# Placing the gates of 256 tokens in a token-by-expert table: element scatters by GpSimd in place of one-hot matmuls

## What is computed

```
u = take(u_tab, expert)                       # (tokens, 8, 16, 2048)
act = gelu(einsum('cd,chkd->chk', x, u))
wgt = gate * act
y = einsum('chk,chkd->cd', wgt, take(v_tab, expert))
x = LN(alpha * x + y)
```

## Time and profile before

| | |
|---|---|
| median of 3 runs | 4104.31 us (4087.92 to 4105.97) |
| the profiled execution's own time | 4092.33 us |
| its span | 4090.4 us |
| mean granted PE clock | 0.974 of full |
| U sweep, first to last Gelu | 2452.2 to 3280.7 us |
| V sweep | 3281 to about 4060 us |
| PE, DVE, ACT, POOL busy | 94%, 67%, 34%, 29% |

### The profile page before, as it was taken

The page is one execution under the profiler, slowest core; times in us unless marked ns, Lnnn a source line. Parts: engine busy times, 40 slices in busy tenths (PEclk is TensorE's granted clock), DMA queues, the critical chain, the costliest instruction groups (busy, mean ns, idle before and its releaser), DMA issues.

```text
span 4090.4 us, 61953 instructions
## 1 busy us (share of the span) xinstructions
PE 3847.7 (94%) x24631; PEld 3529.6 (86%) x24631; DVE 2760.7 (67%) x3403; ACT 1394.6 (34%) x1975; POOL 1181.8 (29%) x595
## 2 busy tenths in 40 slices
PE   7899999999888999999999899999998879999997
PEld 7789999999877788888888799999998867777776
DVE  3444455554675555666555478888887879989889
ACT  4444444443313300000000244466663323433332
POOL 0000000000533344444444262212113334435542
PEclk9899999999999999999999899999999999999998
DMA  4235554455367699999999447999999999999996
GB/s 166 83 107 182 185 184 179 182 184 185 135 260 286 248 402 396 391 406 395 403 397 404 191 160 288 378 366 366 369 364 408 411 400 406 411 400 406 382 399 264
DMA packets 209831, 1240.23 MB, mean 303 GB/s; under 512 B 20176, under 2 KB 53024, under 8 KB 65824
## 3 DMA queue, kind: packets, MB, share of 16 engines
q1 hardware_dynamic: 125024, 663.85, 42.5%
q0 software_dynamic: 73728, 536.90, 32.2%
q10 hardware_dynamic: 10944, 37.75, 2.3%
HBM read 1200.68 MB, written 37.75 MB: 303 GB/s over the span
## 4 chain that ended last, share of the span: by engine, by line
PE 76%; DMA 10%; DVE 8%; ACT 3%; issue 2%; SPq 0%; ACTq 0%; POOL 0%; DVEq 0%
PE dense_ps L850 22%; PE dense_ps L839 12%; PE dense_ps L841 12%; PE dense_ps L840 12%; DMA wbuf<-in_peer_v_dram 5%; PE dense_ps L1046 5%; PE dense_ps L878 3%; DVE h L1084 3%; DMA row<-in_peer_v_dram,expert 2%; PE score_ps L1046 2%; DVE w_lo L1134 2%; PE o_ps L939 1%; PE score_ps L1007 1%; DMA wbuf<-in_w_units_dram 1%; PE o_ps L1046 1%
## 5 line engine op out<-in xcount | busy, mean ns | idle before, releaser
L1134 DVE TENSOR_TENSOR w_lo<-wbuf,w_hi_r 128x1024 fp32r<-128x1024 f32 x804 | 977.9, 1224 | 557.1 <-ACT w_hi_r L528 556.7
L528 ACT ACTIVATE w_hi_r<-wbuf 128x1024 fp32r<-128x1024 f32 x876 | 919.3, 1058 | 1243.7 <-PE dense_ps L841 678.8
L839 PE MATMUL dense_ps<-act_hi,w_hi_r 128*128 128x256 f32 x4160 | 1196.8, 288 | 35.2 <-DVE w_lo L1134 31.5
L840 PE MATMUL dense_ps<-act_lo,w_hi_r 128*128 128x256 f32 x4160 | 1185.6, 285 | 0.0
L841 PE MATMUL dense_ps<-act_hi,w_lo 128*128 128x256 f32 x4160 | 1185.3, 285 | 0.0
L839 PEld LDWEIGHTS dense_ps<-act_hi,w_hi_r 128*128 128x128 f32 x4160 | 806.9, 194 | 47.5 <-DVE w_lo L1134 33.6
L840 PEld LDWEIGHTS dense_ps<-act_lo,w_hi_r 128*128 128x128 f32 x4160 | 807.0, 194 | 0.0
L841 PEld LDWEIGHTS dense_ps<-act_hi,w_lo 128*128 128x128 f32 x4160 | 806.2, 194 | 0.0
L481 POOL DMA_INDIRECT row<-in_peer_v_dram,expert x256 | 529.6, 2069 | 954.8 <-DVE h L1084 925.0
L850 PE MATMUL dense_ps<-xT,wbuf 128*128 128x256 f32 x3200 | 705.4, 381 | 0.7 <-ACT xT L513 0.7
L481 POOL DMA_INDIRECT row<-in_peer_u_dram,expert x256 | 476.7, 1862 | 743.7 <-DVE row L1079 642.2
(11 more groups left out here) (199 smaller groups left out, 4293.0 us busy)
## 6 DMA issues: line engine op xcount, KB each, us to landing
wbuf<-in_w_units_dram SPq DMA_DIRECT2D x460, 1024.0 KB, 5.9
wbuf<-in_peer_v_dram SPq DMA_DIRECT2D x128, 1024.0 KB, 11.3
act_spill<-stage ACTq DMA_DIRECT2D x64, 256.0 KB, 8.1
gate_spill<-gbuf ACTq DMA_DIRECT2D x8, 2048.0 KB, 10.7
e_act<-act_spill SPq DMA_DIRECT2D x32, 512.0 KB, 12.2
e_gate<-gate_spill SPq DMA_DIRECT2D x32, 512.0 KB, 14.1
cT<-in_x_dram SPq DMA_DIRECT2D x2, 2048.0 KB, 10.0
row<-in_peer_u_dram,expert POOLq DMA_INDIRECT x256, 12.2
```

What stands on the lines that cost most here:

```text
L528: act.activation(w_hi[:, j, :], wbuf[n % 2][:, j, :], ACT.Copy).then_inc(w_hi_ready, 1)
L839: nc.tensor.matmul(out, w[0], x[0], start=opens, stop=False)
L840: nc.tensor.matmul(out, w[0], x[1], start=False, stop=False)
L1134: V.tensor_tensor(w_lo[n % 2][:, j, :], wbuf[n % 2][:, j, :], w_hi[:, j, :].bitcast(F32), ALU.subtract).then_inc(lo_by_dve, 1)
```

## The change

The table becomes one DRAM tensor `gate_tab` of 128 x 128 x 256 floats (16.8 MB), laid out as key1, key0, token. In the first half of the tokens, SP fills it with zeros by 16 transfers of 1 MB, one after every fourth unit, from a buffer that GpSimd cleared. DVE makes the element index `spot` of each (token, slot) from the keys with four small instructions. In the U sweep, from unit 4 on, GpSimd issues five `scatter(k)` per unit, 256 in all: each is an indirect DMA that adds one float for each of 128 tokens to the table. The scatters of a head wait until those of the same tile's earlier heads have landed. One-hots, `gate_rows`, `place`, `place_move`, `gbuf`, the transposes and the eight sends go. Five row buffers instead of three serve most of the U sweep, a row is moved from about every eighth unit: the U sweep uses 128 rows where it used 136, and `load_e` reads the gates in runs of 4 KB. SP waits for all scatters before `load_e(0)`, now after the load of unit 57 instead of 55.

```
 def rows_in(n):
     if m >= 0:
-        return 0 if m > 61 else 3 if m % 10 == 0 else 2
+        return 0 if m > 61 else 3 if m % 4 == 0 else 2
     if j >= 0:
-        return 0 if j < 4 else 2 if j < G_FIRST + 32 else 3
+        return 0 if j < 4 else 3 if j % 8 == 7 else 2
...
+PHASES = ((0, (0, 1, 2, 3, 4, 5, 6)), (EARLY_ROWS, (0, 1, 2, 9, 10)), (MID_ROWS, (0, 1, 2)), (LATE_ROWS, (0, 1, 2, 7, 8)))
...
+        gate_tab = nc.dram_tensor("gate_tab", (P * NK * HALF, 1), F32, kind="Internal").ap()
+        gate_rows = gate_tab.rearrange("(p x) o -> p (x o)", p=P)
...
@@ SP, first half of the tokens, after every fourth unit's load
+                    if not b:
+                        sp.dma_start(gate_rows[:, bass.ds(D * i, D)], row[0][:, :]).then_inc(zero_sent, 16)
...
@@ SP, load_e
-                gates = gate_spill[:, :, bass.ds(2 * i + q, 1), :].rearrange("c p o x -> p c (o x)")
+                gates = gate_rows[:, bass.ds((8 * HALF) * i + 4 * HALF * q, 4 * HALF)]
...
-            sp.wait_ge(gate_sent, 16 * (HALF // GCHUNK))
+            for t in range(TILES):
+                sp.wait_ge(spot_sent[t], 16 * SLOTS)
...
@@ POOL
+            def scatter(k):
+                head, t, col = k // (TOPK * TILES), k // TOPK % TILES, k % TOPK
+                at_ = TOPK * head + col
+                if k == 0:
+                    pool.wait_ge(gate_norm, 2 * HALVES)
+                    pool.wait_ge(spot_ready, TILES)
+                if head and col == 0:
+                    pool.wait_ge(spot_sent[t], 16 * at_)
+                pool.indirect_dma_start(
+                    out=gate_tab[:, :], out_offset=bass.IndirectOffsetOnAxis(ap=spot[:, t, at_:at_ + 1], axis=0),
+                    in_=gate[:, 1, t, at_:at_ + 1], in_offset=None, compute_op=ALU.add).then_inc(spot_sent[t], 16)
...
+            for n in range(N_U, N_V):
+                first, count = ROWS_TO[n - 1], ROWS_TO[n] - ROWS_TO[n - 1]
+                k0 = SPOTS_PER * (n - N_U - SPOTS_FIRST)
+                for i in range(3):
+                    for g in range(first + count * i // 3, first + count * (i + 1) // 3):
+                        gather(g)
+                    for k in range(k0 + SPOTS_PER * i // 3, k0 + SPOTS_PER * (i + 1) // 3):
+                        if 0 <= k < U_ROWS:
+                            scatter(k)
...
@@ PE, U sweep
-                    for g in range(G_PER):
-                        place(G_PER * c + g, 4 * G_PER, i)
...
@@ DVE, after the keys of the second half
+                        V.scalar_tensor_tensor(out=key0[t], in0=key1[t], scalar=float(NK), in1=key0[t],
+                                               op0=ALU.mult, op1=ALU.add).then_inc(spot_step, 1)
+                        V.scalar_tensor_tensor(out=spot[:, t, :], in0=key0[t], scalar=float(HALF),
+                                               in1=tok[:, t:t + 1].to_broadcast([P, SLOTS]),
+                                               op0=ALU.mult, op1=ALU.add).then_inc(spot_ready, 1)
```

More of the change, by code:

```diff
@@ L118 @@
 for _g in range(ALL_ROWS):
-    SLOT[_g] = _g % 7 if _g < EARLY_ROWS else (_g - EARLY_ROWS) % 3 if _g < LATE_ROWS else (_g - LATE_ROWS) % 5
-    if SLOT[_g] >= 3 and _g >= LATE_ROWS:
-        SLOT[_g] += 4
+    _first, _slots = [ph for ph in PHASES if ph[0] <= _g][-1]
+    SLOT[_g] = _slots[(_g - _first) % len(_slots)]
     FREE[_g] = _last.get(SLOT[_g], -1) + 1
@@ L323, in build @@
         expert_ready = sem("expert_ready")
-        row_in = [sem(f"row_in{i}") for i in range(9)]
+        row_in = [sem(f"row_in{i}") for i in range(11)]
         row_used = sem("row_used")
@@ L331, in build @@
         out_sent = sem("out_sent")
[L333 to L339, removed]
+        zeroed = sem("zeroed")
+        zero_sent = sem("zero_sent")
+        spot_step = sem("spot_step")
+        spot_ready = sem("spot_ready")
+        spot_sent = [sem(f"spot_sent{t}") for t in range(TILES)]
         act_sent = [sem(f"act_sent{i}") for i in range(4)]
@@ L426, in _ @@
             load_e(1)
-            for j in range(U_UNITS - 8, U_UNITS):
+            for j in range(U_UNITS - 6, U_UNITS):
                 load(N_U + j)
@@ L465, in _ @@
             pool.memset(mask[:, 0, 0:P], NEG).then_inc(masks_ok, 1)
+            pool.memset(row[0][:, :], 0.0).then_inc(zeroed, 1)
+            for t in range(TILES):
+                pool.iota(tok[:, t:t + 1], [[0, 1]], base=t * P, channel_multiplier=1,
+                          allow_small_or_imprecise_dtypes=True).then_inc(masks_ok, 1)
             def low(n):
@@ L492, in _ @@
                 low(n)
-            for g in range(EARLY_ROWS, LATE_ROWS):
+            for n in range(N_U, N_V):
[7 more added lines that the diff above has]
+                            scatter(k)
+            for g in range(ROWS_TO[N_V - 1], LATE_ROWS):
                 gather(g)
@@ L568, in act_unit @@
                     split_hi(n + 2, k)
[L569 to L588, removed]
             def move_e(q):
+                if q == 0:
+                    act.wait_ge(row_used, MID_ROWS + START)
                 act.wait_ge(e_prod, q + 1)
@@ L748, in _ @@
                 act.activation(gate[:, b, :, :], gate[:, b, :, :], ACT.Exp).then_inc(gexp_ready, 1)
[L750 to L770, removed]
+            for j in range(2, U_UNITS):
+                if j == 16:
+                    gathered_act(1)
                 act_unit(j)
@@ L999, in _ @@
                         last.then_inc(ks_ready, 1)
[L1002 to L1009, removed]
             for c in range(8):
                 unit_T(N_U + c, acts)
-            with pe.Fori(0, (IDX_AT - 8) // 4) as i:
+            with pe.Fori(0, (U_UNITS - 8) // 4) as i:
                 for c in range(4):
                     unit_T(N_U + 8 + c, acts, 4, i)
[L1016 to L1027, removed]
-                    for g in range(G_PER):
-                        place(G_PER * c + g, 4 * G_PER, i)
-            with pe.Fori(0, (U_UNITS - G_FIRST - 32) // 4) as i:
-                for c in range(4):
-                    unit_T(N_U + G_FIRST + 32 + c, acts, 4, i)
             def unit_V(m, i=0, opens=False, t_outer=False):
```

55 lines of the change are left out of this document (21 added, 34 removed).

## The result

The changed kernel takes 4201.33 us (median of 4, 4191.13 to 4204.31) against 4105.14 us before: ratio 1.0239, 95% interval 1.0205 to 1.0273. The forecast was 4202, the range 4070 to 4345. The profiled execution took 4191.13 us, span 4189.3, 98.9 us over the one before.

A forecast was written before the change was run, and what follows sets the result against it. PE bounds the U sweep until 3064 us, then DMA, which also bounds the V sweep. 4092.3 + 89 (U sweep) + 7 (V sweep) + 1 (small DVE instructions) = 4189 us profiled, forecast 4202, range 4070 to 4345.

The forecast's parts named there:

- POOL sets the U sweep: U sweep: POOL's indirect DMAs pace each unit at 15.0 us, ending the sweep 89 us later; chance 0.52.
- A scatter priced as a gather: POOL in the U sweep: a scatter also has 128 descriptors, so it costs what a gather does, 1.24 us with DVE idle.
- my feedback formula: U-sweep unit: POOL gets one operation per row instruction and one per 1.24 us of DVE idleness, giving 15.7 us.
- The subtraction as the holder: POOL beside DVE: descriptors are made when DVE is idle or from a row instruction's start; SBUF-to-SBUF subtractions hold them off.
- The 3.40 us: Spacing of indirect DMAs where DVE never pauses; would make 24 us a unit, rejected because DVE waits for POOL's rows.
- Elements hidden on the DMA engines: U sweep: 32,768 single elements at 70 ns make 14.0 us a unit, under POOL's 15.0, so they add nothing.
- The V sweep: V sweep: the moved rows and longer gate runs together cost +7 us, bounds −69 and +21.
- The rows: V sweep: it gets 8 more rows of 1 MB, moved from the U sweep, costing +21 us.
- The runs: V sweep: gates in 4,096 packets of 4 KB instead of 32,768 of 512 bytes give back 14 us, at most 90.
- The end of the U sweep: SP's new wait for the scatters, after unit 57's load, holds nobody long; the U sweep ends at 3370 us.
- Zeros: First half of the tokens: 16 writes of 1 MB cost nothing where PE is full; without that cover, 41 us.
- the free-POOL rival: U sweep: scatters don't queue behind DVE, 11.52 us a unit throughout, −96 us, 4016 us against the median; chance 0.18.

The follow-up runs named there:

- the direct change: Changed kernel with the V sweep's gates read in runs of 512 bytes instead of 4 KB: 4240.93 us, ratio 1.0317 to the kernel before.
- the two single changes: Two runs, each against the changed kernel: V-sweep gates in 512-byte runs (4240.93 us), and the row schedule of the kernel before (4191.12 us).

## Why the prediction was right, and which terms were off

*POOL sets the U sweep: right.* Full POOL, late rows, PE behind DVE, all as described, and halving the scatters removes the whole loss. Forecast 15.0 us a unit, measured 15.4. The U sweep's end was forecast at +89 us and came at +111. PE's share fell to 83%, not to 75%, in part because its matmuls took longer (300 ns on average against 283), at a granted clock of 0.89.

*A scatter priced as a gather: wrong, and covered by another error.* It takes 1.55 us at least, not 0.94, because it adds (0.97 without). With 1.86 in place of 1.24 my feedback formula would have given 9.5 + 5 x 1.86 = 18.8 us, far over 15.4: it let POOL through only once per row while DVE works, and the real hold is smaller, 3.0 to 3.4 us a unit in all. I took the 2.1 us from rows in which gathers stood beside a busy DVE, and they happened to be near the mean of the true mix: 2.03 + 0.30 us a scatter and 1.50 + 0.30 a gather make 2.2.

*The subtraction as the holder: half right.* It holds descriptors off, but for 0.6 us a unit; the row instructions hold them for 2.8. The reading of the earlier trace rows, that descriptors are made from the start of a row instruction and not beside a subtraction, does not hold in the changed kernel, where an operation goes on beside whatever follows the instruction that it began in. In the earlier trace rows the gather was held through a row instruction and the subtraction behind it; why it is held through several there and through one here stays open. The 3.40 us were also the shorter of the gaps there: two of the seven from 3802.56 us on are 6.80. The Trainium skill's rule that a DVE instruction with two SBUF inputs shares a port with GpSimd's reads (SBUF — State Buffer, Who interferes with whom) covers both instructions, and the runs agree: with both cut to 16 columns the pace falls from 15.4 to 12.4 us. The Trainium skill's remark there, marked as inferred, that `tensor_tensor` does not stall the making of descriptors, does not fit this trace: the 60 operations that begin inside a subtraction, which is a `tensor_tensor`, lose 32 us.

*Elements hidden on the DMA engines: right* (64 partitions: 15.1 against 15.4 us; the threshold of the half).

*The V sweep: wrong sign.* Forecast +7, measured −12. The rows were right: 17 to 21 us for 8, forecast 21. The runs were mis-sized: 35 to 39 us, forecast 14, with 90 as the bound. I had taken the rate of another stretch as what runs of 512 bytes cost; the direct change shows about two and a half times that. By the average of 801.3 us the two single changes sum to 21 − 35 = −14 us, and the V sweep is 8 us shorter than the 809.7 before; the 6 us between them are no more than single profiles of the same V sweep differ by (797.4 to 803.7).

*The end of the U sweep: a term of 7 us left out.* SP's wait for the last scatters was forecast to hold nobody long. SP stood in it for 11.7 us, and behind it come the first loads of activations and gates and then the weights of unit 58, for which ACT waited 15.16 us (SP from 3200 us, ACT's timeline):

```profile
SPq L413 <- DMA gate_tab<-gate,spot: 11.7, 1, 11.7
```
```profile
3317.44 2.00 ACT L557 ACTIVATE w_hi_r<-wbuf 128x1024 fp32r<-128x1024 f32 x2 [15.16 <-DMA wbuf<-in_w_units_dram]
```

The Gelus of units 56 and 57 are 21.3 us apart, the last five gaps 11.52 us each. With half the scatters SP has nothing left to wait for, and the same two are 18.5 us apart. So the wait itself cost about 3 us, as forecast, and the loads ahead of the weights 7 us, which the forecast did not have.

*Zeros: right.* The run without scatters keeps them, its first Gelu stands where it stood before (2451.9 and 2452.2 us), and its time is under the free-POOL rival's (3990.5 us; the rival had 4016).

*The sum* of 4189 against 4191 in the profiled execution's terms rests on two misses of opposite sign, 22 us too little in the U sweep and 15 to 19 too much in the V sweep. The mechanism, POOL's pace on the path to PE, was predicted; the closeness was luck, within the U sweep too.

## What to carry to other kernels

Before work is moved to GpSimd's queue, count its indirect DMAs per unit of the loop and price each with the gap before it, as they stand in a row beside a busy DVE: here 2.3 us for an adding scatter of 128 floats and 1.8 for a gather of 1 MB. Their own work is 1.9 and 1.3 us of that; the rest is the time until the DVE instruction in which they begin is over, so one long DVE instruction costs the queue more than short ones of the same sum. A queue that is fed just below its pace costs nothing (2.5 scatters a unit), and twice that costs everything above POOL's capacity, since the gathers behind the scatters are on the path. So split such work and give the queue only the part that fits; here that gained 0.6% over the kernel before.

## What the runs showed of the hardware that was not expected

- An indirect DMA that adds takes POOL 1.55 us beside an idle DVE, one that writes 0.97; with 64 partitions in place of 128 the adding one takes 1.40.
- An indirect DMA that begins inside a DVE instruction with two SBUF inputs ends 0.87 us (gather) or 1.44 us (adding scatter) after the end of that instruction (166 of 172 in the scatter phase); a DVE instruction that begins after it does not lengthen it there.
- The adding scatter leaves 144 packets in POOL's queue (110,592 against 73,728 for 256 of them), the writing one 32 (81,920), the adding one of 64 partitions 80 (94,208).
- In the DMA-bound V sweep, the gates in runs of 512 bytes instead of 4 KB, 28,672 packets more at the same bytes, cost 35 to 39 us.
- PE's granted clock, 1.00 in the placing stretch before, was 0.89 in the same stretch of the changed kernel, where PE kept stopping for a few microseconds: a mean over times at its two levels, 2.4 and 1.2 GHz. As POOL was full there, it should have cost nothing; no run changes the clock alone.
